# First feed-forward matrix as seven products instead of eight, in every block, with five operand sums read back from DRAM

## The reference

```
x = x + mix @ w_out[layer]                      # 1024 -> 1024
h = _rmsnorm(x, norm_ffn[layer])
x = x + jnp.square(jax.nn.relu(h @ w_ff1[layer])) @ w_ff2[layer]   # 1024 -> 4096 -> 1024
```

## Time and profile before

| | |
|---|---|
| median of 3 runs | 2966.64 us (2966.62 to 2966.76) |
| the profiled execution | 2962.78 us |
| its span | 2960.8 us |
| TensorE busy | 2836.6 us (96%), 16334 matmuls |
| VectorE, ScalarE, GpSimd busy | 48%, 32%, 37% |
| TensorE's granted clock, mean | 0.983 |
| DMA | 185.43 MB, mean 63 GB/s |

### The profile page before, as it was taken

One profiled execution on the slowest core, in us unless ns is written; L12 is line 12 of the kernel. 1 busy time (PEld: TensorE's weight loads), 2 busy tenths in 40 slices (PEclk: granted clock), 3 DMA queues, 4 the chain that ended last, 5 costly groups with the idle time before them and its releaser, 6 DMA issues.

```text
span 2960.8 us, 40170 instructions
## 1 busy us (share of the span) xinstructions
PE 2836.6 (96%) x16334; PEld 2598.2 (88%) x16334; DVE 1408.8 (48%) x1836; ACT 933.1 (32%) x1413; POOL 1083.5 (37%) x603
## 2 busy tenths in 40 slices
PE   7999988898999999999999999899999999999998
PEld 7999977686899889998898989887888999889997
DVE  5500236675345476455724310088337645575454
...
GB/s 147 39 38 74 87 117 2 65 122 134 43 15 57 57 43 18 53 57 57 45 37 115 39 129 54 56 59 93 171 15 43 14 57 57 57 36 20 57 64 64
DMA packets 125560, 185.43 MB, mean 63 GB/s; under 512 B 13350, under 2 KB 90498, under 8 KB 124677
## 3 DMA queue, kind: packets, MB, share of 16 engines
...
q10 hardware_dynamic: 132, 0.13, 0.0%
...
## 4 chain that ended last, share of the span: by engine, by line
PE 80%; DVE 8%; issue 5%; ACT 3%; POOL 2%; DMA 1%; PEld 1%; DVEq 0%; PEldq 0%; POOLq 0%; SPq 0%; ACTq 0%
PE ps L481 43%; PE ps L679 14%; PE ps L527 10%; PE ps L759 3%; PE ps L491 3%; DVE units L985 2%; PE ps L1817 1%; PE ps L1798 1%; DVE small L2729 1%; PE ps L424 1%; DVE units L973 1%; DVE units L1004 1%; ACT units L817 1%; PE ps L2134 1%; DMA raw<-w_in_even 1%
## 5 line engine op out<-in xcount | busy, mean ns | idle before, releaser
L481 PE MATMUL ps<-units_r,split 128*128 128x384 f32 x7344 | 1285.8, 335 | 8.7 <-DVEq L287 8.4
L481 PEld LDWEIGHTS ps<-units_r,split 128*128 128x128 f32 x7344 | 1280.4, 189 | 11.7 <-issue 9.5
L919 POOL TENSOR_TENSOR split<-raw,split 128x1024 fp32r<-128x1024 f32 x98 | 268.1, 2745 | 445.1 <-ACT split L820 444.5
L267 POOL TENSOR_TENSOR split<-raw,split 128x2048 fp32r<-128x2048 f32 x38 | 175.6, 4623 | 446.8 <-ACT split L262 446.8
L985 DVE TENSOR_TENSOR units<-units,ps 128x512 f32<-128x512 f32 x434 | 282.5, 681 | 105.4 <-PE ps L679 105.4
L973 DVE TENSOR_TENSOR units<-units 128x1152 f32<-128x1152 f32 x56 | 106.7, 1906 | 450.6 <-ACT units L817 450.6
L679 PE MATMUL ps<-split,units_r 128*128 128x512 f32 x1344 | 313.4, 390 | 1.3
L679 PEld LDWEIGHTS ps<-split,units_r 128*128 128x128 f32 x1344 | 251.2, 188 | 59.0 <-DVE units L985 7.2
L679 PE MATMUL ps<-split,spare_r 128*128 128x512 f32 x1008 | 235.9, 390 | 0.0
L817 ACT ACTIVATE units<-ps 128x1152 f32<-128x1152 f32 x56 | 63.6, 1136 | 544.0 <-PE ps L481 544.0
L679 PEld LDWEIGHTS ps<-split,spare_r 128*128 128x128 f32 x1008 | 189.0, 188 | 38.8
...
## 6 DMA issues: line engine op xcount, KB each, us to landing
...
units<-x_prompt SPq DMA_DIRECT2D x3, 1536.0 KB, 11.9
stream<-units POOLq DMA_DIRECT2D x1, 4608.0 KB, 14.0
units<-park_gv SPq DMA_DIRECT2D x3, 1536.0 KB, 11.7
units<-stream SPq DMA_DIRECT2D x3, 1536.0 KB, 7.3
```

Source lines behind the costliest of these rows:

```text
L267: pool.tensor_tensor(split[:, n % 2, 1, :], raw[:, n % 2, :], split[:, n % 2, 0, :], ALU.subtract).then_inc(lo_ready, 1)
L481: last = pe.matmul(ps[:, bank + n, 0:GN], weights(slab, a, k, c0, P), h[b][:, k, n * GN:(n + 1) * GN], start=(k == 0 and q == 0), stop=(k ...
L919: pool.tensor_tensor(right_slot(base, slot, 1), src, right_slot(base, slot, 0), ALU.subtract).then_inc(lo_ready, 1)
```

## The change

**The first matrix.** The depth is cut in two halves q, the rows in two halves r of 576 (512 prompt rows and 64 sample rows), and the 512 hidden columns of a block in two halves c of 256. Seven products on sums of such quarters replace the eight plain ones. Each is done in two row halves g of 288 rows (row_half): 2 x 4 chunks x 3 passes = 24 matmuls of 288 columns, 14 halves in a block. Some of them are summed on in PSUM (more), and the parts that more than one result needs are copied out by ScalarE (copy) and added by VectorE (hidden_part), which then squares with a maximum in one instruction.

**The operands.** Seven activation operands are needed, and SBUF holds four places, operand(q, r), each 128 x 4608 fp32r with high and low parts. The places (0, 0) and (1, 1) stay. The places (1, 0) and (0, 1) are filled anew: five operands (MIXED, UPPER1, UPPER3, MIXED2, MIXED4), 2304 KB each, are stored in DRAM once in a layer and read back in every block, each when the halves that use the place before are finished (ff_h).

**Where the sums are made.** At the end of the output projection the row tiles come in the order TAIL, so that the tiles of a pair (n, n + 4) follow each other, in five groups (GROUPS; the samples are a group of their own). The turn of position p stands behind the job of position p + 1. VectorE makes four sums of a group out of PSUM (par_tr is the semaphore sums_made, par_ev turned_rows), ScalarE and GpSimd split them, and SyncE stores each in pieces of 128 columns. Three of the four are staged in the slots 2 and 3 of the weights. The barrier is gone: half 1 of the first block stands ahead of the last turn, and in later blocks half 1 of the next stands ahead of a block's end.

**The weights.** They come as quarters of 512 KB. VectorE makes three sums of first-matrix quarters in a block (weight_sums_of), GpSimd one more. GpSimd has 20 operations of 1024 columns in a block where it had 11 and two of 2048.

**The diff**, cut to its core (some parts are only moved together, and `...` marks what is left out):

```diff
+        def operand(q, r, of=pairs_r):
+
+            at = 4 * UNIT * q + QUARTER * r
+            return span(at, at + QUARTER, of).rearrange("p (a k t) -> p a k t", a=2, k=4)
...
+        TAIL = (0, 4, 1, 5, 2, 6, 8, 3, 7)
+        GROUPS = ((0, 1), (2, 3), (4, 5), (6, 6), (7, 8))
+        OUT_JOBS += [(n, 2) for n in range(NARROW)] + [(n, 3) for n in TAIL]
...
+            for g in range(len(GROUPS)):
+                done = SUMS_HI0 + 4 * (len(GROUPS) * layer + g)
+                for c, high in enumerate((2, 3, 4, 4)):
+                    pool.wait_ge(sums_hi, done + high)
+                    c = (1, 0, 2, 3)[c]
+                    pool.tensor_tensor(sum_rows(layer, g, c, 1), sum_values(layer, g, c), sum_rows(layer, g, c, 0), ALU.subtract).then_inc(sums_lo, 1)
...
+            def turn(p):
+                k = 2 * layer + 1
+                xs, _, _ = norm_parts(k)
+                pe.wait_ge(xs_ready, NT * k + p + 1)
+                if p >= 2:
+                    group = [g for g, both_ in enumerate(GROUPS) if p - 2 in both_][0]
+                    pe.wait_ge(sums_made, MADE0 + 4 * (len(GROUPS) * layer + group + 1))
+                for c in range(KC):
+                    last = pe.transpose(turn_banks(p)[:, c], xs[:, p % 2, c * P:(c + 1) * P], ident)
...
-                if kind == 3 and n >= 2:
-                    tile_turn(pe, 2 * layer + 1, n - 2)
-            tile_turn(pe, 2 * layer + 1, NT - 2)
-            tile_turn(pe, 2 * layer + 1, NT - 1)
+                if j > OUT_TAIL:
+                    turn(j - OUT_TAIL - 1)
+            pe.wait_ge(w_add, len(OUT_JOBS) * (layer + 1))
+            pe.wait_ge(turned_rows, ROWS0 + len(GROUPS) * layer + 3)
+            mlp_pe_opening(pe, layer, base + 4, 0, 0)
+            turn(NT - 1)
 
...
+            def sums(g):
+
+                p1, p2 = GROUPS[g]
+                at = tile_columns(TAIL[p1])
+                made = MADE0 + 4 * (len(GROUPS) * layer + g)
+                x1 = turned(p1, FIRST_OF[p1 != p2])
+                x2 = turned(p2, FIRST_OF[1] if p1 != p2 else slice(64, P))
+                dve.wait_ge(norm_hi, NT * k + p2 + 1)
+                if g:
+                    dve.wait_ge(*stored_groups(layer, g - 1))
+                dve.tensor_tensor(sum_values(layer, g, 0), x2[:, 1], sum_values(layer, g, 1), ALU.subtract).then_inc(sums_made, 1)
+                dve.tensor_tensor(sum_values(layer, g, 1), sum_values(layer, g, 1), x1[:, 0], ALU.subtract).then_inc(sums_made, 1)
+                dve.wait_ge(sums_made, made + 1)
+                dve.tensor_tensor(sum_values(layer, g, 2), sum_values(layer, g, 0), x1[:, 0], ALU.add).then_inc(sums_made, 1)
+                dve.tensor_tensor(operand(1, 1)[:, 1, :, at], x2[:, 1], operand(1, 1)[:, 0, :, at],
+                                  ALU.subtract).then_inc(tr_taken, 1 if p1 == p2 else 2)
+                dve.wait_ge(sums_made, made + 3)
+                dve.tensor_tensor(sum_values(layer, g, 3), x1[:, 1], sum_values(layer, g, 2), ALU.subtract).then_inc(sums_made, 1)
+
+            def turned_tile(p):
+                if TAIL[p] < 4 or TAIL[p] == PT:
+                    upper_rows(p)
+                if p in SECOND:
+                    sums(SECOND[p])
+
             for n in range(NT):
...
+            for p in range(NT):
+                add(OUT_TAIL + p)
+                if p >= 2:
+                    turned_tile(p - 2)
+                if p == 0:
+                    dve.wait_ge(gain_in, 16 * (k + 1))
+                scale(p)
+            turned_tile(NT - 2)
+            turned_tile(NT - 1)
...
+        def row_half(pe, base, slot, x, g, bank, more=False):
+
+            for f in range(2):
+                for k in range(4):
+                    for q, (a, b) in enumerate(PASSES):
+                        last = pe.matmul(ps[:, bank + f, 0:HN],
+                                         right_slot(base, slot, a)[:, COLS * k + P * f:COLS * k + P * (f + 1)],
+                                         x[:, b, k, HN * g:HN * (g + 1)], start=(not more and k == 0 and q == 0),
+                                         stop=(k == 3 and q == 2), skip_group_check=more)
+                        begin(last, g == 0 and f == 0 and k == 0 and q == 0)
+            last.then_inc(ff_h, 1)
...
+                pe.wait_ge(turned_rows, ROWS0 + groups * (layer + 1))
+                row_half(pe, base, 0, b21, 1, ROW_BANKS[1])
+                made(3)
+                upper(0)
+                pe.wait_ge(sums_lo, SUMS_LO0 + 4 * (groups * layer + 2) + 1)
+                copied(1)
+                row_half(pe, base, 1, b12, 0, ROW_BANKS[0])
+                pe.wait_ge(sums_lo, SUMS_LO0 + 4 * (groups * layer + 4) + 1)
+                copied(2)
+                row_half(pe, base, 1, b12, 1, ROW_BANKS[1])
+                made(4)
+                pe.wait_ge(sums_made, MADE0 + 4 * groups * (layer + 1))
+                row_half(pe, base, 2, b11, 0, SUM_BANKS[0])
+                row_half(pe, base, 2, b11, 1, SUM_BANKS[1])
+                made(5)
+                mixed(1)
+                for g in range(2):
+                    summed(1 + g)
...
-                right(7)
+                pe.wait_ge(ff_sq, blk * SQUARES + (squares + 15))
+                product(7, ninth(0), 0, True, False, False)
...
+                for r in range(2):
+                    act.wait_ge(stage_out[r][0], stored_groups(layer, len(GROUPS) - r - 1)[1])
+                weight_in(act, layer, 1, 1, blk, 1)
+                weight(blk, 2, right_raw(base, 1, 1), 1)
+                added(1)
+                weight(blk, 3, right_raw(base, 0, 0), 1)
...
+                squared(13)
+                left_high(a2[:, 0], left_third(layer))
+                for g in range(2):
+                    copy(blk, c=1, r=0, g=g, half=13 + g, banks=SUM_BANKS, kind=ACT.Relu)
+                squared(15)
+                left_high(half_of(left_ninth[:, 0, 2:4]), samples_of(plain, 1))
+                left_high(a1[:, 0], quarter(plain, 0, 1))
...
+            def hidden_part(blk, c, r, half, copy, at, banks):
+
+                for g in range(2):
+                    dve.wait_ge(ff_h, blk * ROW_HALVES + (rows + half + g))
+                    dve.wait_ge(ff_relu, blk * COPIES + (copies + copy + g))
+                    part_ = part_of(plain, c, r, g)
+                    dve.tensor_tensor(part_, part_, row_sums(g, banks), ALU.add).then_inc(ff_sq, 1)
+                for g in range(2):
+                    dve.wait_ge(ff_sq, blk * SQUARES + (squares + at + g))
+                    part_ = part_of(plain, c, r, g)
+                    dve.scalar_tensor_tensor(out=part_, in0=part_, scalar=0.0, in1=part_,
+                                             op0=ALU.max, op1=ALU.mult).then_inc(ff_sq, 1)
...
+                for g in range(len(GROUPS)):
+                    sp.wait_ge(turned_rows, ROWS0 + done + g + 1)
+                    straight(MIXED, 1, 0, g)
+                    for count, c in enumerate((1, 0, 2, 3)):
+                        sp.wait_ge(sums_lo, SUMS_LO0 + 4 * (done + g) + count + 1)
+                        if c == 1:
+                            straight(UPPER1, 0, 1, g)
+                        else:
+                            which = {0: UPPER3, 2: MIXED2, 3: MIXED4}[c]
+                            src = stage_place(layer, g, c, pairs_r).bitcast(F32).rearrange("p (m t) -> p m t", m=2 * 4)
+                            stored(which, src, g).then_inc(stored_groups(layer, g)[0], 16)
+                for g in (-2, -1):
+                    sp.wait_ge(*stored_groups(layer, len(GROUPS) + g))
+                sp.wait_ge(straight_out, STRAIGHT0 + 32 * len(GROUPS) * (layer + 1))
+
+                def inside(blk):
+                    made(blk, 5)
+                    quarter_load(layer, base, 1, 1, second_weights(layer, blk, 1, 1))
+                    multiplied(blk, 2)
+                    operand_load(MIXED2)
+                    made(blk, 6)
+                    quarter_load(layer, base, 0, 1, second_weights(layer, blk, 0, 1))
```

758 lines of the change are left out of this document (497 added, 261 removed).

## The result

The changed kernel takes 2985.66 us (median of 4 runs, 2983.44 to 2991.80); the kernel before, beside it, took 2966.63. The ratio is 1.0072, with a 95% interval of 1.006 to 1.0085: 0.7% slower. The forecast was 2982, in a range of 2935 to 3018. The profiled execution took 2983.44 us, with a span of 2981.6.

The account below looks back on a forecast made before the run. TensorE, busy 96% of the span, was taken as the bound. Terms of -77, +57, +14 and +24 us gave +18 on 2962.8, so 2981, or 2985 on the median; 2982 was stated, range 2935 to 3018.

Parts of the forecast that it names:

- A: First matrix: 336 matmuls of 288 columns replace 288 of 384, gaining 4.8 us a block, 77 us in all.
- B: Output projection's end: three waits for VectorE's sums, low clock after each, 19.2 us a layer; extra turn 0.85.
- C: Entry into the first block: waits for stores delay half 7; 9.2 us a layer lost, including the extra turn.
- D: Half 7 of later blocks: second operand's load lands late behind a weight quarter; 1.0 us each, 14 us.
- E: Second matrix, ninth tile: products wait for VectorE's fifteenth square, held by GpSimd; 1.5 us a block, 24 us.
- 1: Rival: the stalls within a block stay hidden; about 2947 us, chance 0.25.
- 4: Rival: waits and saving cancel, within 6 us of before, with in-block stalls of 1.0 to 1.8 us; chance 0.13.
- 2: Rival: stores are quick and the waits at jobs 3, 5 and 7 cost no clock; about 2920 us, chance 0.08.
- 3: Rival: the DMA queues bound a block, fifth operand also late; about 3030 us, chance 0.12.
- The items of the 4.2: Each projection-end wait: VectorE's start 0.2, five steps of 0.6, a last 0.69, TensorE's answer 0.2 us.
- the fifth group follows: Entry into the first block: after the fourth group's turn until 8.6 us, parts end at 19.6, stores at 23.
- The break-even: Per block, stalls at half 7 and at the fifteenth count must sum to over 1.4 us for a slower kernel.

Follow-up runs that it names:

- the last version: Changed kernel with sums ahead of additions, load ahead of quarter, ninth tile waiting for the copy, last groups staged elsewhere, two additions earlier: 2890.66 us, ratio to before 0.9738.
- the fill: Changed kernel with 15 extra matmuls of 512 columns on TensorE ahead of each of turns 2, 4 and 6: 2973.68 us, ratio to before 1.002.
- the moved copy: Changed kernel, but ScalarE copies half 2 of a block ahead of its wait for the staged stores: 3043.47 us, ratio to before 1.0257.
- the shortened sums: Changed kernel, but two of GpSimd's second-matrix weight sums per block do only 16 of 1024 columns, in fourteen blocks: 2952.75 us, ratio to before 0.9954.
- the first experiment: Changed kernel, but at the projection's end VectorE makes a group's sums before the next addition, ScalarE copies them before its square: 2954.09 us, ratio to before 0.9952.

## Why the prediction was right

The sum was +18 us on the profile; what the change did is +16.5. The direction and the mechanisms were right: the columns that are saved are less than what new waits and the clock behind them cost. That the sum is so near is in part luck. The letters stand for the terms of the prediction, and the right column is from the account above, with a gain of 5.44 us in each of sixteen blocks (93.90 - 88.46) taken apart from the waits:

| us, both layers | forecast | profile |
|---|---|---|
| A, fewer columns in the first matrix | -77 | -87 |
| B, the projection's end, with the extra turn | +40 | +41 |
| C, entry into the first block, without that turn | +17 | +26 |
| D and E, stalls at half 7 and in the second matrix | +38 | +36 |

A was 10 us too small a gain and C 9 us too small a loss, and these two errors cancel.

The rivals: 1 and 4 needed stalls of nothing, or of 1.0 to 1.8 us, in a block, and 2.4 us were measured; 2 needed waits without the low clock behind them, and the clock was there; 3 fell with the last version.

**First matrix (A).** Forecast 134.4 ns a matmul and -4.8 us a block. In block 1 it is 44.92 / 336 = 133.7 ns. In the version without these waits a block is 5.4 us shorter. Right, but small: the forecast range for a block, 4.0 to 6.2 us, had it.

**The projection's end (B).** Forecast three waits of 4.2 us with 2.2 us of clock each, 19.2 us a layer, and 0.85 for the turn. Measured 3.87 and 2.2 us, 20.8 and 20.5 with the turn. The items of the 4.2 add up to 4.1. Right in place, cause and size: the other order takes away 16.7 of it, the fill takes away the part behind the wait. The 2.9 us that the first piece lost to the low clock in the kernel before were read a little high: 15.4 us run from TensorE's start to ScalarE's, and that distance is 12.7 in a steady block (1022.44 - 1009.73), so it is 2.7.

**Entry (C).** Forecast half 7 at 39.3 us behind the last job; it came at 44.6. The step that failed is "the fifth group follows": it also stages where the fourth's stores must have landed, which I had left out. It waits until 849.3, 3.7 us longer than for its high parts (845.6), and its own stores landed 4.5 instead of 3.9 us behind the last part. From ScalarE's start on slot 2 (29.4 instead of 24.3) everything is 5 us later. With that wait gone, and the one before it, half 7 comes at 30.7. I also named half 5 as the place of the gap; it stood ahead of half 4, since ScalarE's copy of half 2 is behind the same wait. The moved copy showed that this changes the row and not the time.

**Half 7 of later blocks (D).** Forecast 1.0 us each, 14 us; measured 3.0 us of idle time behind a load in all, 1.5 of it in the first blocks, which belong to C. The mechanism is there and its size was wrong. The load was issued at 10.4 us (958.70 - 948.30, forecast 10.9) and such loads took 8.8 in the median, so it came at 19.2, just when TensorE did, and not at 20.3. Half of this is the earlier issue, half is in the 1.2 us that I had added for the quarter ahead of the load. The margin is real, though: 3 us later in the moved copy gave 3.4 us of waiting and 4 us a block. By the formula of the Trainium skill (DMA: Bandwidth & Descriptors, Anatomy of one DMA), which is fitted to DMAs on GpSimd's path, 2304 KB are an estimate of 7.4 us. The 76 loads here, on SyncE's queue, had a median of 8.8. The 0.2 us a block that went with the 7.4 were nearer to the result than my 1.0, but by a duration that the trace does not show.

**The ninth tile (E).** Forecast 1.5 us a block, 24 in all, by VectorE's row held by GpSimd; measured 25.4. The place and the cause are right, and shown by the shortened sums. What I did not have is that the clock can fall behind this wait: two of twelve blocks were 1.6 and 2.4 us longer. One of them had a wait at half 7 and one had none. Why the clock falls in some blocks and not in others with the same waits stays open; the number of such blocks was 2 of 14 here and 10 of 14 in the profile of the first experiment.

**The break-even** was 1.4 us a block for D and E together. A block without waits gains 5.4 us and the steady blocks gained 35.8 / 12 = 3.0, so the waits and the clock behind them took 2.4, as the forecast's 2.5 had it. Nearly all of the 2.4 is at the ninth tile, where the forecast had 1.0 of the 2.5 at half 7. The change is slower.
